# Value transposes of the next prompt chunk ahead of the output transposes of the finished one, in a hybrid decoder layer step

## The reference, cut to what matters

```python
x = x + 0.5 * swiglu_1(rmsnorm(x))
z = rmsnorm(x) @ w_in                         # q, k, v and gates of 4 mLSTM and 4 GLA heads
x = x + concat(mlstm(z), gla(z)) @ w_out      # linear attention with carried states
x = x + cross_attention(rmsnorm(x), memory)   # 4 heads, 256 memory tokens
x = x + 0.5 * swiglu_2(rmsnorm(x))
y = rmsnorm(x)
```

```python
s   = (q @ k.T) * W                               # W from the gates, causal
num = s @ v + w_inter * (q @ C)
den = s.sum(2) + w_inter * (q @ n)
h   = num / max(abs(den), exp(-m))
y   = sigmoid(mo) * head_rmsnorm(h)
C, n = iL * C + (wL * k).T @ v, iL * n + (wL * k).sum()
```

## Time and profile before

| | |
|---|---|
| three timed executions | 1359.83, 1360.73, 1365.76 us, median 1360.73 |
| the profiled execution, its own time | 1365.62 us |
| its span in the profile | 1363.8 us |
| TensorE busy, share of the span | 98% |
| VectorE, ScalarE, GpSimd busy | 49%, 31%, 3% |
| mean granted TensorE clock, as a share of full speed | 0.987 |
| stretch with the four prompt chunks | about 619 to 675 us from the span's start |

### The profile page before, as it was taken

One profiled execution on the slowest core, in us unless ns is written; L12 is line 12 of the kernel. 1 busy time (PEld: TensorE's weight loads), 2 busy tenths in 40 slices (PEclk: granted clock), 3 DMA queues, 4 the chain that ended last, 5 costly groups with the idle time before them and its releaser, 6 DMA issues.

```text
span 1363.8 us, 25703 instructions
## 1 busy us (share of the span) xinstructions
PE 1332.1 (98%) x10995; PEld 1294.7 (95%) x10995; DVE 665.6 (49%) x903; ACT 429.4 (31%) x644; POOL 41.7 (3%) x64
## 2 busy tenths in 40 slices
PE   7999999999999999998899999999999999999997
PEld 7999999999999999998798898889999999999997
DVE  4554455433333366667666534535454454443332
ACT  6222222222222143245533623324322222222221
POOL 1000000000000000002111000100000000000000
PEclk8999999999999899999899999999999999999998
DMA  6323323323333223224035773533323323323221
GB/s 196 94 80 89 92 81 88 88 74 95 87 74 93 78 79 78 79 78 125 13 115 164 225 238 124 187 139 93 93 79 91 92 80 89 92 74 94 87 70 66
DMA packets 208136, 138.31 MB, mean 101 GB/s; under 512 B 6550, under 2 KB 196224, under 8 KB 208068
## 3 DMA queue, kind: packets, MB, share of 16 engines
q1 hardware_dynamic: 200240, 109.88, 28.0%
q0 software_dynamic: 7664, 27.27, 5.8%
q10 hardware_dynamic: 164, 0.16, 0.0%
HBM read 129.41 MB, written 7.88 MB: 101 GB/s over the span
## 4 chain that ended last, share of the span: by engine, by line
PE 49%; DVE 1%; ACT 0%; issue 0%; ACTq 0%
PE ps L1688 47%; PE ps L2124 1%; PE ps L2228 0%; ACT prob L871 0%; PE ps L2153 0%; DVE xmx L1561 0%; PE ps L2074 0%; DVE kT L1578 0%; PE ps L2102 0%; ACT kT L882 0%; DVE y_raw L1399 0%; DVE prob L1570 0%; DVE q_pad L1643 0%; DVE yf_s L1679 0%; DVE acc L976 0%
## 5 line engine op out<-in xcount | busy, mean ns | idle before, releaser
L1688 PE MATMUL ps<-xn_hi,w_hi 128*128 128x272 f32 x2144 | 449.5, 291 | 2.9 <-ACT xn_hi L573 2.9
L1688 PE MATMUL ps<-xn_hi,w_lo 128*128 128x272 f32 x2144 | 446.3, 289 | 0.0
L1688 PE MATMUL ps<-xn_lo,w_hi 128*128 128x272 f32 x2144 | 445.0, 288 | 0.0
L551 ACT ACTIVATE w_hi<-raw 128x1024 fp32r<-128x1024 f32 x206 | 217.9, 1058 | 650.8 <-PE ps L1688 650.8
L965 DVE TENSOR_TENSOR w_lo<-raw,w_hi 128x1024 fp32r<-128x1024 f32 x206 | 252.4, 1225 | 200.8 <-ACT w_hi L551 199.8
L1688 PEld LDWEIGHTS ps<-xn_hi,w_hi 128*128 128x128 f32 x2144 | 338.5, 190 | 4.2 <-DVE w_lo L965 3.1
L1688 PEld LDWEIGHTS ps<-xn_hi,w_lo 128*128 128x128 f32 x2144 | 339.7, 190 | 0.0
L1688 PEld LDWEIGHTS ps<-xn_lo,w_hi 128*128 128x128 f32 x2144 | 337.9, 190 | 0.0
L1688 PE MATMUL ps<-h_hi,w_hi 128*128 128x272 f32 x704 | 146.0, 289 | 0.0
L1688 PE MATMUL ps<-h_hi,w_lo 128*128 128x272 f32 x704 | 145.5, 288 | 0.0
L1688 PE MATMUL ps<-h_lo,w_hi 128*128 128x272 f32 x704 | 145.1, 287 | 0.0
(11 more groups left out here) (345 smaller groups left out, 1087.6 us busy)
## 6 DMA issues: line engine op xcount, KB each, us to landing
raw<-in_ffn_w_gate SPq DMA_DIRECT2D x44, 512.0 KB, 3.8
raw<-in_ffn_w_up SPq DMA_DIRECT2D x44, 512.0 KB, 3.8
raw<-in_w_in SPq DMA_DIRECT2D x29, 512.0 KB, 3.8
raw<-in_ffn_w_down SPq DMA_DIRECT2D x32, 448.0 KB, 3.7
raw<-in_ffn_w_down SPq DMA_DIRECT2D x16, 512.0 KB, 4.0
kv<-in_cache_mem_k POOLq DMA_DIRECT2D x6, 1024.0 KB, 7.1
kv<-in_cache_mem_v POOLq DMA_DIRECT2D x6, 1024.0 KB, 6.9
raw<-in_w_out SPq DMA_DIRECT2D x8, 512.0 KB, 3.9
```

What stands on the lines that cost most here:

```text
L551: act.activation(w_hi[u0 % 2][:, :], raw[u0 % 4][:, :], ACT.Copy).then_inc(sem("hi_done"), 1)
L1688: return pe.matmul(out, lhsT, rhs, start=start, stop=stop)
```

## The change

In TensorE's loop over the chunks two calls change places: `values(c + 1)` is issued ahead of `back(c)` and no longer behind it. For c = 0, 1 and 2 the ten transposes of `values` with their three waits stand ahead of the eight of `back` with their two. For c = 3 there is no `values`, and nothing changes. No instruction is added or removed, and the streams of the other engines and the DMAs stay as they are.

```diff
                     scores_and_keys(c + 1)
                 else:
                     sample_tokens()
-                back(c)
                 if c + 1 < NC:
                     values(c + 1)
+                back(c)
 
 
             sample_heads()
```

## The result

| | before | after |
|---|---|---|
| median of 18 timed executions each | 1363.25 us | 1366.22 us |
| lowest and highest | 1359.83, 1368.29 | 1363.31, 1369.38 |
| ratio after to before | | 1.0023, 95% interval 1.0013 to 1.0033 |
| the profiled execution, and its span | 1365.62, 1363.8 us | 1363.31, 1361.4 us |

By the ratio the change costs 3.1 us (0.0023 of 1363), with an interval of 1.8 to 4.5 us; the two medians differ by 2.97. 2.7 were forecast. The first three executions of before, which the prediction had, gave a median of 1360.73; with 15 more of them it is 1363.25, so the forecast of 1363.4 was the right difference on a base that was 2.5 us too low.

A forecast was written before the change was run, and what follows sets the result against it. TensorE, busy 98% of the span, was taken to bound the kernel. Gates delayed by 0.90 us in each of three chunks sum to 2.7 us, giving 1363.4 us from 1360.73, range 1360.0 to 1367.5.

The forecast's parts named there:

- What ends the cycle: TensorE's outputs of the next chunk wait for VectorE's gates, which need the transposes of `back`; TensorE idles 1.42 us before them.
- The 0.90 us a chunk: Chunks 0 to 1 and 2 to 3: gates slip 0.90 us, as `back` queues behind `q_in` and four GLA value transposes.
- Chunk 1 to 2: Cycle partly at 1.2 GHz, where `back` already ends last: gates 0.90 us later, with 0.65 and 1.4 as ends.
- the lower end, 0.65: Chunk 1 to 2 at the full clock: gates at 649.64, 0.65 us later than before the change.
- about 0.8 us in all three cycles: Sign of being right: VectorE idle about 0.8 us between `p_done` and the gates, released by TensorE, in all three cycles.
- What gives nothing back: Values reach PSUM up to 1 us earlier, but ScalarE copies them only after the keys, so nothing is regained.
- rival 2: Earlier values shorten the cycle if ScalarE's copies decide when outputs start: 3.5 us gained, 1357.2 us; chance 0.04.
- Rival 1: The delay of `back` is hidden in TensorE's idle time before outputs and nothing moves: 1360.7 us; chance 0.08.
- The rule about weight loads: TensorE may pull the first load of `back` past the waiting GLA value transposes, making the sum some 0.3 us smaller.
- Rival 3: TensorE's clock falls more often between keys and outputs, at most 1.7 us a stretch; one or two 0.10, three on 0.07.
- the upper end of 1.4: Chunk 1 to 2 at the low clock: transposes of 0.215 us put the gates at about 650.4, 1.4 us later.
- The base: The median before the change that the forecast added its 2.7 us to: 1360.73 us.

## Why the prediction was right, point by point

**What ends the cycle** was read rightly: gates release outputs, `back` releases gates, and the 1.42 us that TensorE waits ahead of the outputs hid nothing. The releasers after the change are the ones named.

**The 0.90 us a chunk.** At the full clock the sum came out within 0.01 us and its parts within 0.05: `q_in` ends at 642.95, the GLA values start at 643.00, `back` at 643.39 and the gates at 644.57, 1.62 us behind `q_in` where 1.61 was the sum. The cycles cost 0.92, 0.93 and 1.00 where the clock was equal on both sides, in the runs with split spreads. The wait makes 0.47 of it, as measured by itself, and the four transposes behind it the rest, half of what eight more of them cost (0.86).

**Chunk 1 to 2**, the one with unequal ends, cost 13.40 - 12.78 = 0.62 between the two profiled executions, since before had the low clock there and after had not: the lower end, 0.65. Chunk 2 to 3 went the other way: 12.47 at the full clock before, 14.16 after with low clock over the transposes, 1.69 more. Chunk 0 to 1 changed by -0.09 (12.58 before, with low clock over the outputs of chunk 0; 12.49 after, with it over the transposes). Their sum is 2.2 us (the other 0.4 of the stage's 2.59 lie behind chunk 3), and where the clock falls in an execution decides which cycle pays what. So the sign "about 0.8 us in all three cycles" held in one of them. That 2.7 lies so near the measured 3.1 is in part luck: the interval runs from 1.8 to 4.5 us, and how much of the 3.1 is the order at the full clock and how much its price at the low clock, no run separates.

**What gives nothing back** held. `v_tok` started at 643.92, right behind the key copies that began at 642.92, though its values had been in PSUM since before 642.2; no releaser of outputs is ScalarE, and rival 2 falls. Rival 1 falls by VectorE's idle time ahead of the gates and by the ratio, whose interval leaves out 1.

**The rule about weight loads** did neither harm nor good. In the rows of the cycle after the change, the first load of `back` begins at 643.39, one load ahead of its matmul (643.50), while the last GLA value transposes run, but none passed the transposes that waited for `q_in_done` at 642.95. The load one ahead agrees with what the Trainium skill says in "TensorE: Matmul & The Clock Gate", section "Step-by-step: what each phase is for", that TensorE pulls weight loads ahead of matmuls in flight. Whether a load may pass a matmul that waits on a semaphore the page leaves open; here the 0.3 us that this would have saved did not show.

**Rival 3, the clock**, was weighed wrongly in kind, though not in the sum. I priced it as additional stretches at 1.7 us each. The changed stage had no more low clock than before (about 6.8 us lost in both). But what a stretch costs depends on where it falls: over the transposes it takes the margin that hid `back`. The prediction had this for chunk 1 to 2 alone, as the upper end of 1.4, and had no such term for the other two. The runs give its size: the cycle with such a stretch is 14.16 us long after the change and 12.78 before, 1.38 more, where at the full clock the order costs 0.93. It may also be why a move that is free at the full clock (eight transposes ahead) measured 1.0024; that is argued, not shown.

**The base** was the largest error: three executions, one of them 5 us above the others, set the median 2.5 us low. The resolution of 0.5% that the prediction assumed was too coarse: with 18 executions of each kernel the interval is 0.1% to either side.

## What to carry to other kernels

An engine's stream holds everything behind a wait. Before moving work ahead of a step, write down when each of its waits ends and compare this with the slack of the step, taken from the rows: the end of `back` had 1.2 us, its start was forecast to move by 2.06, and the difference, 0.86, was the price at the full clock to 0.1 us. And take that slack at the lower clock as well, because a margin that is there at 2.4 GHz can be gone at 1.2 GHz. Where executions scatter by more than the effect, compare the same cycle in traces with the same clock.

## What the runs showed of the hardware

- Splitting the two spreads of gate rows by the `q k` products left 1 fall of the clock in the 12 cycles of four traces, counting from the outputs of chunk 0 on and without falls over those outputs themselves. In nine traces with the spreads in one piece there were 13 in 27 cycles (one or two in seven of the traces). From the start of the spreads to each of the 13 falls TensorE was busy without a break; what it did was 2 us of products with four input partitions, then up to 1.1 us of `q k` products. The fall at 461.8 us in the kernel before also came without idle time, behind 2.1 us of products with 16 input partitions and during those with 32. The same spreads passed without a fall in the other 14 cycles, so they do not make one by themselves. The mean granted clock over the stage, on the order of before, rose from 0.88 to 0.94:

```profile
622.32:678.51 56.19, 49.85 (x501) 44.94 (x502) 38.56 (x124) 30.01 (x126) 7.98 (x14) 0.94 0.21 57
```

  Only half of that rise belongs to the split: of the two stretches that are missing, one lay over the outputs of chunk 0, ahead of the first split spread. That the total time hardly moved (0.9998) was not expected. The cycles give a reason: on the order of before, a stretch between two chunks made the cycle 0.31 us longer (12.78 against 12.47), so there was little to win, and falls elsewhere, as around 462 us, vary from one execution to the next.
- A transpose of 128 x 128 took 0.108 us at 2.4 GHz and 0.215 at 1.2 GHz, one behind the other. TensorE resumed 0.05 to 0.06 us after VectorE's last write of `q_in` and of `ew`, and 0.15 us after that of the gates ahead of the outputs (645.86 to 646.01); why these differ is open.
